# Gate and up projections of two gated networks by seven block products in place of eight, on one Trainium2 core

## What is computed

```python
D_MODEL = 1024
SEQ = 512
D_FF = 2816
def swiglu(x, wg, wu, wd):
    return (jax.nn.silu(x @ wg) * (x @ wu)) @ wd
...
    h = h + 0.5 * swiglu(rmsnorm(h, ffn1_norm[i]), ffn1_wg[i], ffn1_wu[i], ffn1_wd[i])
...  # attention of two kinds
    h = h + 0.5 * swiglu(rmsnorm(h, ffn2_norm[i]), ffn2_wg[i], ffn2_wu[i], ffn2_wd[i])
```

## Time and profile before

| | |
|---|---|
| median of 3 runs | 2104.66 us (2102.88 to 2106.46) |
| span of the profiled execution | 2100.9 us |
| TensorE busy in it | 2065.8 us, 15692 matmuls |
| mean granted TensorE clock | 0.996 |
| DVE, ACT, POOL busy | 854.1, 717.4, 907.5 us |
| read from and written to memory | 179.03 MB by DMA, mean 85 GB/s |

### The profile page before, as it was taken

The page is one execution under the profiler, slowest core; times in us unless marked ns, Lnnn a source line. Parts: engine busy times, 40 slices in busy tenths (PEclk is TensorE's granted clock), DMA queues, the critical chain, the costliest instruction groups (busy, mean ns, idle before and its releaser), DMA issues.

```text
span 2100.9 us, 37982 instructions
## 1 busy us (share of the span) xinstructions
PE 2065.8 (98%) x15692; PEld 1788.4 (85%) x15692; DVE 854.1 (41%) x1254; ACT 717.4 (34%) x1085; POOL 907.5 (43%) x690
## 2 busy tenths in 40 slices
PE   8999999999999999999999999999999999999998
PEld 7888888877887888887888999999999898998887
DVE  4222300577686522223008527833221546555202
ACT  5222221445687422224215432331222432222213
POOL 4444444435321444344444534435443154445542
PEclk9999999999999999999999999999999999999999
DMA  5323222431100223322322232122322123232221
GB/s 183 98 81 100 100 89 91 139 115 61 42 4 3 91 80 100 100 87 93 100 100 80 81 100 63 62 81 80 100 84 83 35 81 97 83 100 89 91 100 60
DMA packets 152360, 179.03 MB, mean 85 GB/s; under 512 B 7109, under 2 KB 142766, under 8 KB 152254
## 3 DMA queue, kind: packets, MB, share of 16 engines
q1 hardware_dynamic: 152091, 177.43, 26.0%
q10 hardware_dynamic: 163, 0.04, 0.0%
HBM read 175.37 MB, written 2.10 MB: 84 GB/s over the span
## 4 chain that ended last, share of the span: by engine, by line
PE 72%; issue 13%; POOL 8%; DVE 5%; ACT 2%; DMA 1%; SPq 0%; POOLq 0%; DVEq 0%; ACTq 0%
PE ps L2061 47%; PE ps L2202 11%; POOL wlo L734 8%; PE ps L2709 2%; PE ps L2472 1%; PE ps L2503 1%; PE ps L2483 1%; PE ps L2303 1%; DVE tmp L1396 1%; DMA raw<-in_ffn_wu 1%; DVE Q L1880 0%; DVE K L1883 0%; PE ps L2510 0%; PE ps L2610 0%; PE ps L2560 0%
## 5 line engine op out<-in xcount | busy, mean ns | idle before, releaser
L734 POOL TENSOR_TENSOR wlo<-raw,whi 128x512 fp32r<-128x512 f32 x630 | 841.8, 1368 | 1068.0 <-ACT whi L830 1067.9
L2061 PE MATMUL ps<-xh,whi 128*128 128x258 f32 (+2 forms) x2400 | 687.3, 333 | 1.0 <-POOL wlo L734 0.7
L2061 PE MATMUL ps<-xh,wlo 128*128 128x258 f32 (+2 forms) x2400 | 682.0, 331 | 0.0
L2061 PE MATMUL ps<-xl,whi 128*128 128x258 f32 (+2 forms) x2400 | 680.3, 330 | 1.4 <-issue 1.4
L830 ACT ACTIVATE whi<-raw 128x2048 fp32r<-128x2048 f32 (+1 forms) x158 | 301.3, 1907 | 770.0 <-PE ps L2061 479.3
L2061 PEld LDWEIGHTS ps<-xh,whi 128*128 128x128 f32 x2400 | 406.7, 189 | 52.5 <-issue 3.1
L2061 PEld LDWEIGHTS ps<-xh,wlo 128*128 128x128 f32 x2400 | 405.6, 188 | 45.3 <-issue 1.9
L2061 PEld LDWEIGHTS ps<-xl,whi 128*128 128x128 f32 x2400 | 405.4, 189 | 45.4 <-issue 1.6
L2202 PE MATMUL ps<-act_h,wlo 128*128 (+1 forms) x528 | 208.6, 395 | 0.0
L2202 PE MATMUL ps<-act_l,whi 128*128 (+1 forms) x528 | 208.6, 395 | 0.0
L2202 PE MATMUL ps<-act_h,whi 128*128 (+1 forms) x528 | 208.6, 395 | 0.0
(11 more groups left out here) (358 smaller groups left out, 2324.9 us busy)
## 6 DMA issues: line engine op xcount, KB each, us to landing
raw<-in_w_in SPq DMA_DIRECT2D x47, 1024.0 KB, 5.0
raw<-in_ffn_wu SPq DMA_DIRECT2D x22, 1024.0 KB, 5.3
raw<-in_ffn_wd SPq DMA_DIRECT2D x22, 1024.0 KB, 4.9
raw<-in_w_up SPq DMA_DIRECT2D x22, 1024.0 KB, 5.1
raw<-in_ffn_wg SPq DMA_DIRECT2D x21, 1024.0 KB, 5.3
raw<-in_w_down SPq DMA_DIRECT2D x11, 1024.0 KB, 4.9
raw<-in_w_out SPq DMA_DIRECT2D x8, 1024.0 KB, 5.0
raw<-in_ple_w_gate SPq DMA_DIRECT2D x4, 1024.0 KB, 4.9
```

The source lines that it names most:

```text
L734: last = nc.gpsimd.tensor_tensor(wlo[:, slot, d], raw[:, slot, d], whi[:, slot, d].bitcast(F32), ALU.subtract)
L2061: last = mm(ps[:, j * banks + b, 0:n], w[:, k, e * P:(e + 1) * P], x[:, k, c0:c0 + n], start=(k == 0 and q == 0), stop=(k == KD - 1 and q ...
```

## The change

The twenty units behind the first two are multiplied by Strassen's scheme, one level, in the variant with seven products and shared sums. A unit (1024 rows by 256 columns) is cut into 2x2 blocks of 512 rows by 128 columns, the activations into 2x2 blocks of 512 rows by 256 tokens. In place of eight block products (48 matmuls 512 wide) there are seven, each with 4 row blocks by three products, 256 wide: 84 matmuls. The sums that this needs are:

- of the weights, four block sums a unit (j = 1, 2, 4, 5) by DVE (`seven_sum`), written where `wlo` will be (`wsum`). ACT then rounds seven pieces of 512, and POOL makes six rests of 512, DVE the seventh (`seven_rest`, j = 5)
- of the activations, four sums of 128x1024 a network (`x_sums`), rounded by ACT (`sums_rounded`) with rests by DVE (`x_rests`). They are made from `xf`, a float32 copy of x times the gain, eight instructions of ACT (`xf_of`)
- of the results: ACT keeps three partial sums a unit (`kept`), DVE combines them in five instructions (`seven_taken`), the last of which multiplies by `rbs`. Silu, product, rounding and rest are now made for two tiles at once, 1024 wide, once in two units

`whi` and `wlo` become rings of eight pieces, seven to a unit, and a piece is free when TensorE has finished the product that used it. Since room is short, the inner width is done in two passes: 12 tiles (the two opening units and ten units), six down units, DVE adds the eight banks to `h` (`half_added`), then ten units and five down units. The second network's embedding of `p` moves ahead of its last five down units. The loops are written out.

The core of the diff:

```diff
+HI_ORDER = (0, 3, 1, 2, 4, 5, 6)
+LO_ORDER = (0, 3, 1, 2, 4, 6)
...
+        self.kinds = ["open"] * 2 + ["seven"] * 10 + ["down"] * 6 + ["seven"] * 10 + ["embed"] * embed + ["down"] * 5
...
+            def seven_lo(f, u):
+                for j in LO_ORDER:
+                    if j in (1, 4):
+                        pool.wait_ge(piece_sum, PIECE_SUM[u, SUMS[SUMS.index(j) + (2 if j == 1 else 1)]])
+                    pool.wait_ge(*rounded_piece(f, u, j))
+                    src = raw_block(u, *RAW_OF[j]) if j in RAW_OF else block_of(wsum_f, f, u, j)
+                    nc.gpsimd.tensor_tensor(block_of(wlo_f, f, u, j), src, block_of(whi_f, f, u, j).bitcast(F32),
+                                            ALU.subtract).then_inc(lo_ready if j == LO_ORDER[-1] else piece_lo, 1)
...
+            def xf_of(n, gain):
+                nc.scalar.activation(xf[:, n, :], h[:, n, M:T], ACT.Copy, scale=col(gain, n)).then_inc(xf_ready, 1)
+            def sums_rounded(f):
+                act.wait_ge(sum_made, 16 * f.g + 4)
+                for i in range(4):
+                    nc.scalar.activation(sumh[:, i], sums[:, i], ACT.Copy).then_inc(xf_ready, 1)
...
+            def seven_period(f, k):
+                u = f.sevens[k]
+                i = (k + 2) // 2 if k % 2 else k // 2
+                more = f.kind(u + 1) == "seven"
+                d = f.downs[0 if k < 10 else 6]
+                if more:
+                    seven_hi(f, u + 1, 0)
+                kept(f, k, 0)
+                if not more and f.kind(u + 1) == "down":
+                    down_hi(f, d, 0)
+                kept(f, k, 1)
+                if more:
+                    seven_hi(f, u + 1, 3)
+                elif f.kind(u + 1) == "down":
+                    down_hi(f, d, 1)
+                else:
+                    embed_hi(f, u + 1)
+                if k % 2:
+                    silu_pair(f, (k + 1) // 2)
+                if more:
+                    seven_hi(f, u + 1, 1)
+                    seven_hi(f, u + 1, 2)
+                if k % 2 == 0 and k not in (0, 10):
+                    acth_pair(f, k // 2)
+                kept(f, k, 2)
+                if more:
+                    for j in (4, 5, 6):
+                        seven_hi(f, u + 1, j)
...
             for n in range(KD):
                 square_of(0, n, h[:, n, M:T], M)
-            hi_one(2)
+            for n in range(KD):
+                xf_of(n, "ffn1_norm")
+            sums_rounded(FFNS[0])
+            for j in (0, 3, 1, 2):
+                seven_hi(FFNS[0], 2, j)
...
-            nc.scalar.activation(h[:, :, 0:M], ps[:, 4, 384:384 + KD * M].rearrange("p (n m) -> p n m", n=KD), ACT.Copy).then_inc(meta_ready, 1)
...
+            def seven_rest(f, u):
+                for j in range(7):
+                    if (u, j) in PIECE_REST:
+                        dve.wait_ge(*rounded_piece(f, u, j))
+                        nc.vector.tensor_tensor(piece(wlo_f, f, u, j), piece(wsum_f, f, u, j), piece(whi_f, f, u, j).bitcast(F32),
+                                                ALU.subtract).then_inc(piece_rest, 1)
+            def x_sums(f):
+                part = lambda row, half: xf[:, 4 * row:4 * row + 4, half * HS:(half + 1) * HS]
+                t = [sums[:, i] for i in range(4)]
+                n0 = 16 * f.g
+                dve.wait_ge(xf_ready, (KD + 4) * f.g + KD)
+                nc.vector.tensor_tensor(t[0], part(0, 1), part(0, 0), ALU.subtract).then_inc(sum_made, 1)
+                nc.vector.tensor_tensor(t[1], part(1, 1), part(0, 1), ALU.subtract).then_inc(sum_made, 1)
+                dve.wait_ge(sum_made, n0 + 1)
+                nc.vector.tensor_tensor(t[2], part(1, 1), t[0], ALU.subtract).then_inc(sum_made, 1)
+                dve.wait_ge(sum_made, n0 + 3)
+                nc.vector.tensor_tensor(t[3], part(1, 0), t[2], ALU.subtract).then_inc(sum_made, 1)
+            def x_rests(f):
+                for i in range(4):
+                    dve.wait_ge(xf_ready, (KD + 4) * f.g + KD + i + 1)
+                    nc.vector.tensor_tensor(suml[:, i], sums[:, i], sumh[:, i].bitcast(F32), ALU.subtract).then_inc(sum_made, 1)
+            def opened(f):
+                g, t0 = f.g, tile0(f.first)
+                for j in range(2):
...
+                for j in range(2):
+                    dve.wait_ge(tiles_done, t0 + 2 + j + 1)
+                    nc.vector.tensor_tensor(tmp[:, 2 + j, 0:S], ps[:, 2 + j, :], rbs[:, M:T], ALU.mult).then_inc(up_scaled, 1)
+                    if j:
+                        seven_sum(f, f.sevens[0], 4)
+                    dve.wait_ge(gate_done, FT * g + j + 1)
+                    dve.wait_ge(up_scaled, FT * g + j + 1)
+                    nc.vector.tensor_tensor(tmp[:, 2 + j, 0:S], tmp[:, j, M:T], tmp[:, 2 + j, 0:S], ALU.mult).then_inc(prod_done, 1)
+                    if j:
+                        seven_sum(f, f.sevens[0], 5)
+                    dve.wait_ge(acth_done, FT * g + j + 1)
+                    nc.vector.tensor_tensor(actl2[:, j, :], tmp[:, 2 + j, 0:S], acth2[:, j, :].bitcast(F32), ALU.subtract).then_inc(actl_done, 1)
...
+            def seven_taken(f, k):
+                v = 20 * f.g + k
+                u = f.sevens[k]
+                b, q = 4 * (v % 2), sc[:, v % 2]
+                dst = tmp[:, 2:4, 0:S] if k % 2 else tmp[:, 0:2, M:T]
+                dve.wait_ge(seven_kept, 3 * v + 2)
+                nc.vector.tensor_tensor(q[:, 1, :], q[:, 1, :], q[:, 2, :], ALU.add).then_inc(seven_step, 1)
+                dve.wait_ge(seven_done, 6 * v + 4)
+                nc.vector.tensor_tensor(dst[:, 0, 0:HS], ps[:, b + 1, 0:HS], q[:, 0, :], ALU.add).then_inc(seven_step, 1)
+                dve.wait_ge(seven_kept, 3 * v + 3)
+                dve.wait_ge(tiles_done, used_count(u))
+                s0 = dst[:, 0, HS:HS + 1]
+                cross = bass.AP(tensor=s0.tensor, offset=s0.offset, ap=[s0.ap[0], [T - HS, 2], [1, HS]])
+                nc.vector.tensor_tensor(cross, ps[:, b + 2:b + 4, 0:HS], q[:, 3, :].unsqueeze(1).to_broadcast([P, 2, HS]), ALU.add).then_inc(seven_step, 1)
+                dve.wait_ge(seven_step, 4 * v + 1)
+                nc.vector.tensor_tensor(dst[:, 1, HS:S], q[:, 1, :], q[:, 3, :], ALU.add).then_inc(seven_step, 1)
+                dve.wait_ge(seven_step, 4 * v + 4)
+                nc.vector.tensor_tensor(dst, dst, rbs[:, M:T].unsqueeze(1).to_broadcast([P, 2, S]), ALU.mult).then_inc(up_scaled if k % 2 else gate_scaled, 2)
+            def prod_pair(f, i):
+                dve.wait_ge(gate_done, FT * f.g + 2 * i + 2)
+                dve.wait_ge(up_scaled, FT * f.g + 2 * i + 2)
+                nc.vector.tensor_tensor(tmp[:, 2:4, 0:S], tmp[:, 0:2, M:T], tmp[:, 2:4, 0:S], ALU.mult).then_inc(prod_done, 2)
+            def actl_pair(f, i):
+                t = 2 * i % UPS[0]
+                dve.wait_ge(acth_done, FT * f.g + 2 * i + 2)
+                nc.vector.tensor_tensor(actl2[:, t:t + 2, :], tmp[:, 2:4, 0:S], acth2[:, t:t + 2, :].bitcast(F32), ALU.subtract).then_inc(actl_done, 2)
+            def seven_period(f, k):
+                u = f.sevens[k]
+                more = f.kind(u + 1) == "seven"
+                old = k not in (0, 10)
+                if old:
+                    seven_taken(f, k - 1)
+                seven_rest(f, u)
+                if old and k % 2 == 0:
+                    prod_pair(f, k // 2)
+                if more:
+                    for j in (1, 2, 4):
+                        seven_sum(f, u + 1, j)
+                if old and k % 2 == 0:
+                    actl_pair(f, k // 2)
+                if more:
+                    seven_sum(f, u + 1, 5)
+            def seven_end(f, k):
+                seven_taken(f, k)
+                prod_pair(f, (k + 1) // 2)
+                actl_pair(f, (k + 1) // 2)
...
+            def ffn(f):
+                opened(f)
+                for k in range(10):
+                    seven_period(f, k)
+                seven_end(f, 9)
+                for j in (1, 2):
+                    seven_sum(f, f.sevens[10], j)
+                half_added(f, 0, 4)
+                for j in (4, 5):
+                    seven_sum(f, f.sevens[10], j)
+                half_added(f, 4, KD)
+                dve.wait_ge(sum_made, 16 * f.g + 16)
+                for k in range(10, 20):
+                    seven_period(f, k)
+                    if f.embed and k == EMBED_AT[1] + 1:
+                        embedding_rest()
+                seven_end(f, 19)
...
+            x_sums(FFNS[0])
+            for j in (1, 2):
+                seven_sum(FFNS[0], 2, j)
+            x_rests(FFNS[0])
             rsqrt(0, 1)
             keep_spread(0, True)
...
+            def seven(f, k, made, embed=None):
...
+                    pe.wait_ge(up_scaled, FT * f.g + 2)
+                    made()
+                elif k in (10, 11):
+                    pe.wait_ge(sum_made, 16 * f.g + 8 + 4 * (k - 9))
+                else:
```

(15 more changed lines are left out.)

504 lines of the change are left out of this document (382 added, 122 removed).

## The result

| | before | changed |
|---|---|---|
| median of the runs | 2104.48 us (2102.88 to 2106.46) | 2181.42 us (2180.26 to 2182.51) |
| ratio | 1 | 1.0362, 95% interval 1.0348 to 1.0377 |
| span of the profiled execution | 2100.9 us | 2178.9 us |
| TensorE busy | 2065.8 us | 2053.8 us |
| mean granted clock | 0.996 | 0.986 |

The changed kernel is 3.6% slower. The forecast was 2200 in a range of 2150 to 2245; the time came out 19 us under the forecast and inside the range.

The account below looks back on a forecast made before the run. It took DVE and POOL, which hold each other up, to replace TensorE as the bound. 2100.9 + 65 (runs of units) + 23 (first start) + 8 (second start) = 2197, with 3.8 us around the span 2200; range 2150 to 2245.

Parts of the forecast that it names:

- The bound: Seven-product units: DVE and POOL, taking turns, become the bound at 24.4 us for two units; TensorE needs 9.95 a unit.
- The price of a turn: Units: a DVE instruction with two SBUF inputs adds 0.97 us to POOL's row for 1024 columns, 0.46 for 512, 0.20 for 256.
- 13.0 a unit: Seven-product units not prepared ahead: 13.0 us each, from 26 us for two by following the four engines' written order.
- the floor: Rival for the units: DVE and POOL interleave without gaps, 12.2 us a unit, +36 us, total 2165; chance 0.20.
- +65 for the runs: Four runs of ten units: 508 us against 443, nine units a run at 13.0 and the first prepared ahead.
- Start of the first network, +23: Before the first network's units: TensorE pauses of 11.4 and 5.6 us, 1 us for sum and rests, 5 for the clock.
- Root late: First network's start: ACT's root stands behind copies, sums and rounding, so TensorE stands still 11.4 us before the spread.
- Fourth tile: First network's start: the first seven-product unit waits 5.6 us for DVE to take the fourth opening tile, no longer hidden.
- Start of the second, +8: Second network's start: spread 2.9 us late, then the fourth-tile chain 2.8, first rests 1.3 less 0.9, clock 2.
- TensorE stays the bound: Rival for the units: sums and rests overlap better, 9.95 us a unit, -45 us, total 2083; chance 0.08.
- The clock in the runs: Rival: TensorE's pauses in every second unit bring half clock, total 2231 to 2261; chance 0.18, shared with a longer chain.
- What would show it: Profile signs: POOL's rests at 1.6 to 1.8 us, block sums over 1, TensorE waiting for L879 and L1786, no DVE/POOL pause.

Follow-up runs that it names:

- e2: Changed kernel with POOL writing zeros in place of its six weight rests in all forty seven-product units, that part left out: 2086.38 us, ratio 0.9905.
- e3: Changed kernel with the seventh rest of each unit (piece 5) moved from DVE to POOL: 2199.59 us, ratio 1.0445.
- e10: Changed kernel with the scaling L1845 reading PSUM instead of `rbs` in 32 of 40 units, the norm's factor left out there: 2155.72 us, ratio 1.0245.
- e12: Changed kernel, full computation, with as many DVE instructions as possible (scalings, products, rests, last sums) given one PSUM operand: 2120.94 us, ratio 1.0071.
- e11: Changed kernel with POOL writing zeros in place of its six rests in the odd units alone, that part left out: 2101.48 us, ratio 0.9982.
- e5: Changed kernel with the norm's factor taken off the up tiles and put on the down product in PSUM: 2182.88 us, ratio 1.0374.

## Why the prediction was right, and where its sizes were off

**The bound.** It said that with seven products TensorE gives the bound away to DVE and POOL, which hold each other up wherever DVE reads two SBUF tensors. e2, e3, e10 and e12 show this. It took the bound as a sum, POOL's rests and what DVE adds to them; the table of pairs shows a narrower one, DVE's row as the rests stretch it, while POOL is idle for 5.4 us of 25.5. The sum is 1.1 us under the pair in the changed kernel, but 4.2 under in e11 (16.9 for 21.06), so it isn't the rule of the bound, and that so close a number came of it is in part luck. TensorE's own price was right: 0.1185 us a matmul, 9.95 a unit; 0.117 and 9.8 were measured.

**The price of a turn.** 0.97 us for 1024 columns was read from one stretch of the trace of before; the runs give 0.97 (e10) and 1.12 (e5), and e12's six instructions together come to within 0.1 us. For instructions of POOL's the prices don't hold so well: 1.0 us for 1.6 in e3, 4.4 for 7.6 in e11. The Trainium skill ("SBUF — State Buffer", section "SBUF: two separate sides") has the pair of ports locked for the whole instruction, which with the recorded duration of 1.21 us gives, as an estimate, two times 1.21, 2.4 us a pair in e10; 1.93 was measured. Its condition, two SBUF inputs on DVE's side against a GpSimd instruction that reads SBUF, is what e10 and e2 show.

**13.0 a unit.** It is 12.74 in the steady part, 0.54 above the floor of 12.2. The prediction got its 0.8 above the floor from four sources added by eye; what the trace shows is a DVE row that is never empty but for 1.1 us in two units, while it waits for ACT's rounding. The same 1.0 to 1.1 a pair above the sum of the turns is seen in the changed kernel (25.47 on 24.4), e10 (23.54 on 22.5), e12 (21.13 on 20.1) and, at 0.9, in e5, where DVE's waiting for ACT is 1.1 each time; in e3 it is 0.5, in e11 4.2.

**+65 for the runs.** Measured +49.6 (23.3 + 26.3). The term was mis-sized by 0.26 a unit too much for 36 units, 9 us; by the second run of the first network, which took 120.9 where the prediction's form with the measured pace gives 124.6, since its first unit took 9.3 us up to its first L1834, for 13.1 in the first run with that start's waits and half clock in it; and by the forty units of before, 445 us for 443.

**Start of the first network, +23.** 18.3 came. Root late: 11.4 said, 9.5 measured. The eight copies ended at 31.0, as said (30.9), and the root was done 0.6 us sooner than said (43.35); the larger part is that TensorE itself came to this place at 34.1 and not at 32.8, and its lateness is in the 18.3 just the same. Fourth tile: 5.6 said, 5.45 measured. The rest is the clock, said to be 5 us for the two pauses. The stretch about the start:

```profile
36.00:60.00 24.00, 10.94 (x51) 9.90 (x52) 14.57 (x18) 13.66 (x23) 7.20 (x5) 0.67 0.01 2
```

A granted clock of 0.67 means the half level (1.2 GHz) for 2 x 0.33 x 24 = 16 us, more than foreseen, but TensorE was busy for only 10.9 of the 24, so much of it fell on its standstill. Ahead of the first product it cost some 2 us (from spread to product took 7.5 us more than before, 5.45 of it the wait); behind it the first 25 matmuls came every 0.22 us for 0.117, 2.4 us more, which are counted in the run.

**Start of the second, +8.** 3.1 came. The spread was not late. DVE was done with the sums and their rests 16.9 us after its start on them (776.5 to 793.4), for 18.2 said, with six rests of POOL's beside them as said; TensorE had itself lost 2.0 us to POOL's rests ahead of its second unit, a wait that the prediction doesn't have, and so it didn't have to wait for the spread. Another 1.35 stand ahead of the first product, less 0.9 for the transposes. The clock did not fall; where it does, in nine of the other kernels, the start is 2 to 4 us longer.

**Not foreseen: +6.9 in the second block**, which the change doesn't touch. It made up for part of what the other terms had too much, 15.4 + 4.7 + 4.9 us: without it the time would have been 2174.5, still in the range but 25 under the forecast. That much is luck. (One sum of the prediction is off by 2: with the starts hidden as well the bound by TensorE gives 2060, not 2062.)

**The rivals.** The floor was worth more than its 0.20: its pace of 12.2 missed 12.74 by 0.54 and the forecast's 13.0 by 0.26, but its time, 2165, is 16 us under the result and the forecast 19 over. "TensorE stays the bound" fell to the first window. The clock in the runs: granted 0.93, 1.00, 1.00 in three pairs, so it fell in the first, and as long as DVE holds the pace it cost nothing there, since the pair takes 25.47 either way.

**What would show it**: nearly all of it did, the mean of POOL's rests 1.77 and 1.57 us, block sums over 1 us in three of four (1.02, 1.02 and 1.79 in the mean, the fourth 0.78), TensorE waiting for L879 and L1786. Only "POOL and DVE together without pause" was too strong: POOL has pauses of 5.4 us in a pair.

## What to carry over

Before TensorE is relieved of work by sums on other engines, add up for one period what DVE does and what POOL's reading instructions add to its instructions with two SBUF inputs (here 0.8 us a rest), not the two engines as parallel rows, and hold it against TensorE's time with the work taken away. Where DVE is the one that is held, move an operand to PSUM before reordering: here the operand's place brought 60 us, and three reorderings 0, 3 and 3, none of them clear of the noise. Take a wait's name as the last link only; measure a loop by its period, since the distance from its first to its last matmul can shrink with nothing gained.

## What the runs showed of the hardware that I had not expected

- A DVE instruction of 256 columns with two SBUF inputs takes up to 1.52 us beside POOL's rests, a little less than to wait for one of them (1.25) and then run (0.41 alone). In proportion the small ones suffer most.
- What DVE's instructions cost can be added up: two less with two SBUF inputs gave 1.93 us, six gave 4.34, both within 0.1 us of the sum of prices read from two stretches of another part of the kernel. With POOL's rests the same sum failed by up to 3.2 us.
- TensorE stopped for up to 4.0 us in a dense row of 32-column matmuls while a block of its instructions was loaded, and went on 2.4 to 3.0 us after the block's packet in all 56 such waits. The 24 waits over 1.5 us all have a load of weights right ahead of that packet. The same 2178 matmuls took 79.2 to 87.5 us over all the kernels here, so differences of under 8 us between kernels, even with the same stream of instructions (up to 4), can come from this alone.
